# A streaming encoder step on one core: three normalizations, half a choice of experts and two sample steps moved to other places

## The reference

```
h = RMSNorm(x);  z = h @ w_in          # q, k, v of two attentions, forget logits, two gates
o_A = DiffAttn(...); o_B = FoX(...)    # 8 heads each; softmax over earlier frames
x = x + (sig(g_A)*(o_A @ w_pa) + sig(g_B)*(o_B @ w_pb)) @ w_o
# PEER on h2 = RMSNorm(x):
q = h2 @ wq; sc = q . subkeys          # 8 heads x 2 lists of 128 scores
top 16 of each list -> 256 sums -> top 16 of these, softmax g
act = gelu(u[e] . h2);  x = x + sum_e g*act*v[e]     # 128 experts (rows of u and v) per frame
y = RMSNorm_final(x)
```

## Time and profile before

| | us |
|---|---|
| median of 3 runs (2168.32 to 2173.65) | 2169.91 |
| profiled execution | 2172.85 |
| its span | 2171.0 |
| busy: PE / DVE / POOL / ACT | 1649.2 / 1504.9 / 750.6 / 542.9 |
| mean rate of transfers over the span | 347 GB/s |

### The profile page before, as it was taken

The page is one execution under the profiler, slowest core; times in us unless marked ns, Lnnn a source line. Parts: engine busy times, 40 slices in busy tenths (PEclk is TensorE's granted clock), DMA queues, the critical chain, the costliest instruction groups (busy, mean ns, idle before and its releaser), DMA issues.

```text
span 2171.0 us, 22161 instructions
## 1 busy us (share of the span) xinstructions
PE 1649.2 (76%) x7163; PEld 1035.9 (48%) x7163; DVE 1504.9 (69%) x3350; ACT 542.9 (25%) x1451; POOL 750.6 (35%) x697
## 2 busy tenths in 40 slices
PE   7878889898878766988868667977886665666555
PEld 6777886375456522764466323535673222222211
DVE  1121207687877798458976898876789997888786
ACT  2233012111621222145601223733022210001011
POOL 0000000354333334334433334333254455554552
PEclk9988899999979987999989988987999888788878
DMA  7743564799999988999899988897999899999996
GB/s 229 264 140 97 202 229 162 291 421 396 423 369 421 421 347 344 370 387 347 331 417 421 419 300 362 333 410 298 420 379 421 330 413 410 422 421 421 422 403 275
DMA packets 129395, 753.79 MB, mean 347 GB/s; under 512 B 16992, under 2 KB 33296, under 8 KB 42880
## 3 DMA queue, kind: packets, MB, share of 16 engines
q0 software_dynamic: 78336, 570.46, 65.0%
q1 hardware_dynamic: 28432, 155.19, 19.1%
q10 hardware_dynamic: 22512, 26.73, 3.6%
HBM read 732.32 MB, written 19.48 MB: 346 GB/s over the span
## 4 chain that ended last, share of the span: by engine, by line
PE 38%; DMA 25%; DVE 25%; issue 6%; ACT 4%; POOL 1%; ACTq 0%; SPq 0%; DVEq 0%; POOLq 0%; PEldq 0%
DMA ring<-in_uv,stage 17%; PE pz L1249 8%; PE pz L1260 8%; DVE ring L1998 7%; PE acc L1598 7%; DVE vsum L2025 3%; DMA wbuf<-in_w_o 2%; DVE F L1875 2%; PE ps L1556 2%; PE ps L1501 2%; DMA wbuf<-in_w_q 2%; DMA wbuf<-in_w_pa 1%; DMA zt_joint<-F 1%; DVE F L1870 1%; PE ps L1521 1%
## 5 line engine op out<-in xcount | busy, mean ns | idle before, releaser
L804 POOL DMA_INDIRECT ring<-in_uv,stage x544 | 692.9, 1274 | 998.8 <-DVE vsum L2025 350.7
L1598 PE MATMUL acc<-ring,diag 128*128 128x512 f32 (+1 forms) x1112 | 623.0, 707 | 293.0 <-DVE diag L2009 202.9
L1998 DVE CUSTOM_DVE_ANT_0 ring<-ring,xb 128x1024 f32<-128x1024 f32 x544 | 649.3, 1221 | 95.0 <-DMA ring<-in_uv,stage 92.8
L1598 PEld LDWEIGHTS acc<-ring,diag 128*128 128x128 f32 (+1 forms) x1112 | 226.5, 217 | 651.8 <-DVE diag L2009 295.4
L2025 DVE SCALAR_TENSOR_TENSOR vsum<-ring,coefd,vsum 128x1024 f32<-128x1024 f32 x261 | 335.7, 1286 | 10.4 <-DVE coefd L2016 1.2
L1126 ACT ACTIVATE gel<-dots 128x1 f32<-128x1 f32 x544 | 102.0, 200 | 921.1 <-DVE dots L1998 907.0
L822 POOL COPY stage<-idx 128x4 int32<-128x4 int32 x136 | 54.9, 404 | 393.4 <-DVE gw L1944 392.6
L1249 PE MATMUL pz<-F,wbuf 128*128 128x128 f32 (+1 forms) x896 | 171.8, 351 | 9.8 <-PE pz L1249 4.8
L1249 PEld LDWEIGHTS pz<-F,wbuf 128*128 128x128 f32 x896 | 141.9, 200 | 40.0 <-issue 16.0
L2016 DVE TENSOR_SCALAR coefd<-gel,gw 128x1 f32<-128x1 f32 x266 | 55.8, 210 | 111.5 <-ACT gel L1126 111.2
L1260 PE MATMUL pz<-wbuf,F 128*128 128x256 f32 (+1 forms) x384 | 85.0, 381 | 1.9 <-PE pz L1260 1.9
(11 more groups left out here) (381 smaller groups left out, 1943.1 us busy)
## 6 DMA issues: line engine op xcount, KB each, us to landing
wbuf<-in_w_z SPq DMA_DIRECT2D x58, 1024.0 KB, 7.1
wbuf<-in_w_q SPq DMA_DIRECT2D x32, 1024.0 KB, 9.8
wbuf<-in_w_pa SPq DMA_DIRECT2D x16, 1024.0 KB, 10.0
wbuf<-in_w_o SPq DMA_DIRECT2D x16, 1024.0 KB, 10.3
ring<-in_uv,stage POOLq DMA_INDIRECT x544, 12.2
wbuf<-in_w_pb SPq DMA_DIRECT2D x16, 512.0 KB, 8.8
wbuf<-in_w_sk SPq DMA_DIRECT2D x4, 1024.0 KB, 11.0
zt_mid<-F ACTq DMA_DIRECT2D x18, 128.0 KB, 5.3
```

Of the source, the lines that this page charges most:

```text
L804: pool.indirect_dma_start(out=ring[:, slot, :], out_offset=None, in_=d["uv"], in_offset=bass.IndirectOffsetOnAxis(ap=stage[:, a, k:k + 1], ...
L1598: last = nc.tensor.matmul(acc[0:nq, c * 512:(c + 1) * 512], diag[:, parity, 0:nq], ring[:, slot, D + c * 512:D + (c + 1) * 512], start=Fal ...
L1998: nc.vector.tensor_tensor_reduce(out=u, in0=u, in1=xb[:, t % 2, :], scale=1.0, scalar=0.0, op0=ALU.mult, op1=ALU.add, accum_out=dots[:, sl ...
```

## The change

Four parts.

1. Opening. The normalizations and transposes of tiles 2, 3 and 4 leave the opening and stand behind pieces 16 to 19 of tile 0's front (TURN_O and the first three of YPROJ). In the opening only tile 1's stays. TensorE's transposes of tiles 2 to 4 now also wait for the copies of tile 0's attention output, since they use the same two banks.
2. Filling of tile 0's front. The eight gate chunks stand behind pieces 1, 2, 4, 6, 8, 10, 12, 14 (were 0, 2, 4, 6, 8, 10, 11, 13). Of the six query chunks two stand behind pieces 15 and 25, the others behind 35 and later (were 16, 21, 26, 31, 36, 38). EARLY is 3: of group 1's chunks one less (a key chunk) is done before tile 0's slots and one more beside them.
3. Choice of experts of tile 3 in halves. top(3, i) works on four of the eight heads in the front, and the other four are an event late_top between half blocks 2 to 22 of tile 3's own slots; GpSimd and VectorE wait for it before half block 32. The sample's choice moves from half blocks 2 to 42 to 26 to 56. A new area class JointTop lays two halves out.
4. Sample. Piece 4 does step 2, piece 5 step 3, the latter with other banks (ps[0] and pz[0] instead of po); the results are scaled one piece later.

```diff
-EARLY = 4
+EARLY = 3
...
-        return 1.5 if what == "front" and p >= TOP else 1.0
+        return 1.0
...
-    norms = [("bias", 0, 0)]
-    for t in range(1, TILES):
-        norms += [("norm_h", t, 0)] + ([("load_x", t + 1, 0)] if t + 1 < TILES else []) + [("turn_h", t, 0)]
...
+    behind = {0: [("bias", 0, 0)], 1: [("norm_h", 1, 0), ("load_x", 2, 0)], 6: [("turn_h", 1, 0)]}
+    for n, i in enumerate(GROUP_ITEMS[HEADS:]):
+        plan += [("project", 0, i)] + behind.get(n, [])
+
+    gates, queries, keys = ([("project", g, i) for i in items]
+                            for g, items in ((2, GATE_ITEMS), (4, QUERY_ITEMS), (1, KEY_ITEMS[:EARLY])))
+    beside_front = {NORM_O: queries[:1], NORM_X: queries[1:2],
+                    TURN_O: [("norm_h", 2, 0), ("load_x", 3, 0)],
+                    YPROJ: [("turn_h", 2, 0), ("norm_h", 3, 0), ("load_x", 4, 0)],
+                    YPROJ + 1: [("turn_h", 3, 0), ("norm_h", 4, 0)],
+                    YPROJ + 2: [("turn_h", 4, 0), ("keep_h", 1, 0)]}
+    for n, part in enumerate(spread(gates, lambda e: 1.0, NORM_O)):
+        beside_front[n + 1] = part + beside_front.get(n + 1, [])
+    for n, part in enumerate(spread(queries[2:] + keys, lambda e: 11.8 if e[1] == 1 and e[2] else 5.0, PIECES - SCORE)):
+        beside_front[SCORE + n] = part
...
-        if 2 <= b < 2 + 4 * 11 and b % 4 == 2:
-            plan.append(("sample_top", TILES - 1, b // 4))
+        if 2 <= b < 2 + 2 * 11 and b % 2 == 0:
+            plan.append(("late_top", JOINT, b // 2 - 1))
+        if 26 <= b < 26 + 3 * 11 and b % 3 == 2:
+            plan.append(("sample_top", TILES - 1, (b - 26) // 3))
...
+        def sample_tail(u):
+            return ps[0] if u == 3 else po
+        def sample_out(u):
+            return pz[0] if u == 3 else po
...
+                if b == SLOTS // BLOCK // 2 and h == 0 and t == JOINT:
+                    pool.wait_ge(route_ready, t + 2)
...
+                if t > 1:
+                    pe.wait_ge(oT_stored, 3)
...
-                    pe.wait_ge(h_stored, 8 * TILES)
+                    pe.wait_ge(h_stored, 8 * 2)
...
-                elif p == 4:
-                    for u in (2, 3):
-                        turn(u)
-                        pv(u)
+                elif p in (4, 5):
+                    turn(p - 2)
+                    pv(p - 2)
...
-                a, heads = (fa(t), HEADS) if t <= JOINT else (top_s, HEADS // 4)
+                a, heads = (fa(t), HEADS) if t < JOINT else (top_j[half], HEADS // 2) if t == JOINT else (top_s, HEADS // 4)
+                turn = t + half if t <= JOINT else t + 1
```

More of the change, by code:

```diff
@@ L197, in make_plan @@
         plan += [("project", 0, GROUP_ITEMS[i]), ("toeplitz", i, 0)]
-    norms = [("bias", 0, 0)]
-    for t in range(1, TILES):
-        norms += [("norm_h", t, 0)] + ([("load_x", t + 1, 0)] if t + 1 < TILES else []) + [("turn_h", t, 0)]
[L201 to L215, removed]
+    behind = {0: [("bias", 0, 0)], 1: [("norm_h", 1, 0), ("load_x", 2, 0)], 6: [("turn_h", 1, 0)]}
[12 more added lines that the diff above has]
+        beside_front[SCORE + n] = part
+    for p in range(PIECES):
+        plan += [("front", 0, p)] + beside_front.get(p, [])
     for t in range(JOINT):
@@ L536, in build @@
         top_s = SampleTop(F, qT[:, D:D + 4 * P])
+        top_j = [JointTop(F, half) for half in range(2)]
         def fa(t):
@@ L1001, in sample @@
                 u = p - 2
-                for v in (u,) if u in (0, 1) else (2, 3) if u == 2 else ():
+                for v in (u,) if 0 <= u < 4 else ():
                     act.wait_ge(turned, 16 * t + v + 1)
@@ L1444, in pv @@
                                 cols, v_ = slice(0, DVB), vb[0:w, j, h * DVB:(h + 1) * DVB]
-                            last = nc.tensor.matmul(po[DEC * i:DEC * i + DEC, cols],
+                            last = nc.tensor.matmul(sample_out(u)[DEC * i:DEC * i + DEC, cols],
                                                     joint.aTS[0:w, P * j + DEC * i:P * j + DEC * i + DEC], v_,
@@ L1938, in top @@
                                                         a.e12[:, 1, :], ALU.mult, ALU.add))
-                    step(nc.vector.tensor_copy(idx[:, par, 0:slots], a.e12[:, 0, :]))
-                    dve.wait_ge(g_exp, t + 1)
+                    here = slice(half * slots, half * slots + slots)
+                    step(nc.vector.tensor_copy(idx[:, par, here], a.e12[:, 0, :]))
+                    dve.wait_ge(g_exp, turn + 1)
                     gexp = a.cand[:, :, 1, :]
@@ L1943, in top @@
                     step(nc.vector.reciprocal(sstat[:, 0:heads], sst[:, 0:heads]))
-                    nc.vector.tensor_tensor(gw[:, par, 0:slots].rearrange("p (h s) -> p h s", h=heads), gexp,
+                    nc.vector.tensor_tensor(gw[:, par, here].rearrange("p (h s) -> p h s", h=heads), gexp,
                                             sstat[:, 0:heads].rearrange("p (h o) -> p h o", o=1)
@@ L2045, in experts @@
             def experts(t, b, h):
+                if b == SLOTS // BLOCK // 2 and h == 0 and t == JOINT:
+                    dve.wait_ge(route_ready, t + 2)
                 if b == 0 and h == 0:
-                    dve.wait_ge(route_ready, t + 1)
+                    dve.wait_ge(route_ready, t + 1 if t <= JOINT else t + 2)
                     if t == TILES - 1:
@@ L2080, in _ @@
                     sample(p)
+                elif what == "late_top":
+                    top(t, p, 1)
                 elif what == "sample_top":
```

61 lines of the change are left out of this document (37 added, 24 removed).

## The result

The changed kernel takes 2136.85 us in the median of 4 runs (2130.67 to 2143.72) against 2169.17 of before (now also 4 runs): ratio 0.985, 95% interval [0.9825, 0.9875], so 32.5 us (27 to 38) are gone where 15 were forecast. The profiled execution took 2134.4 us, its span is 2132.6, the mean clock 0.903.

The account below looks back on a forecast made before the run. TensorE and chains of small waits bound the time before the first slot, then DMA transfers at about 421 GB/s. Terms 7 + 5 + 3 = 15 us off 2172.85 gave 2157.9, median forecast 2155, range 2135 to 2171.

Parts of the forecast that it names:

- Choice in halves: Tile 3's choice: 8 of 12 us idle transfers regained in tile 2's slots, 5 lost in tile 3's, net 3.
- Opening: Before tile 0's front: moving the transposes of tiles 2 to 4 and unblocking tile 1's saves 10.0 us.
- First attention step: Tile 0's front: qT's load, now bare, costs 5.9 us; of the opening's 10.0 us, 4.9 are left.
- Normalizations beside the output projection: Tile 0's front: query chunk fills a wait, 4 us saved; moved transposes and waits cost more, net about 1 lost.
- Fillings: Query chunks moved from between OPROJ and SCORE to behind SCORE: net 11.3 us saved, about 2 of new waiting.
- Key chunk: One more key chunk beside tile 0's slots: 2.5 us lost if transfers decide, 11.7 if TensorE; taken as 6.
- rival A: Transfers decide everything later: key chunk costs 2.5, sample gives 9, halves 12, tile 3 loses nothing; 2138 us, chance 0.2.
- Sample: Sample's steps in tile 2's slots: both VectorE scaling waits go, 5 us gained of at most 16.4.
- Tile 3's slots: The late half of the choice in tile 3's slots, where VectorE has 23 us idle: 5 us lost (0 to 27).
- rival C: Late half makes VectorE the bound of tile 3's first 44 slots: 12 us slower than before, 2182 us, chance 0.08.

Follow-up runs that it names:

- experiment 4: Changed kernel with tile 3's choice whole again and a choice piece's weight back at 1.5: ratio 0.9952 to the kernel before, 22 us slower than the changed kernel.
- experiment 1: Changed kernel with only a choice piece's weight back at 1.5 in tile 2's list: ratio 0.9888 to the kernel before, 8 us slower than the changed kernel.
- experiment 3: Kernel before with tile 3's choice in halves and the sample's choice later, weight 1.5 kept: ratio 0.9971, 6.3 us faster than before.
- experiment 2: Changed kernel with tile 3's choice whole again, weight 1 kept: ratio 0.9913 to the kernel before, 13.7 us slower than the changed kernel.
- experiment 8: Changed kernel with the sample's piece 4 doing steps 2 and 3 again: ratio 0.9868 to the kernel before, 3.9 us slower than the changed kernel.
- experiment 10: Changed kernel with the first gate chunk behind piece 0 instead of piece 1 of tile 0's front: ratio 0.9821 to the kernel before, median 2131.85 us.
- the repetition: The changed kernel run once more, unchanged: ratio 0.9843 to the kernel before, tile 2's slots 408.3 us.

## Why the prediction was wrong in size

The step that failed is "Choice in halves": 8 of 12 us gained in tile 2's slots, 5 lost in tile 3's, net 3. Undoing the whole part costs 22 us of device time (experiment 4); in the traces tile 2's slots change by 22 us and tile 3's by 3, net 19. That is 16 to 19 us more than the net 3, where 17 were missing.

Two things were wrong in the step. First, I priced only the choice's own 60 us, with 12 us of idle transfers, and the sample's 40 us, with 16; tile 2's slots had 54 us of idle transfers in all, 19 of them in their first quarter, to which the sum gave nothing. Second, the edit also sets a choice piece's weight from 1.5 to 1, and I gave that no term: it takes the choice from fifteen half blocks to eleven and spreads attention, sample and projections over four more. That saves 8 us of device time, and 9 to 17 in the stage ahead of the choice (experiments 1 and 4). How the rest divides is open: halves give net 5 to 6 on the list of before (experiment 3), but 14 by device time on the even list (experiment 2).

The other terms, one by one:

- **Opening**, 10.0 forecast, 7.5 in these two executions, 9.2 if counted from the load of the bias. I wrote that nothing but ScalarE's copies holds the next chunk. The copy itself stands on ScalarE behind the root of tile 1's normalization, which waits for VectorE, which waits for the load of the bias. In the profile after, and the load in the one before:

```profile
77.10 0.48 DVE L1738 MEMSET bias<- 64x512 f32 x1 [52.73 <-DMA bias<-skew]
77.51 0.09 DVE L1701 TENSOR_SCALAR sst<-sst 128x1 f32<-128x1 f32 x1
77.64 0.20 ACT L878 ACTIVATE sstat<-sst 128x1 f32<-128x1 f32 x1 [4.92 <-DVE sst L1701]
```

```profile
75.40 0.48 DVE L1708 MEMSET bias<- 64x512 f32 x1 [51.36 <-DMA bias<-skew]
```

The transposes left TensorE's way; the normalization did not leave ScalarE's. The same wait already stood ahead of the 76.05 that I started from, so it is not what the sum missed: the load ended 1.7 us later in this execution. Over all traces it ends between 72.6 and 77.5 us with the new opening and between 75.4 and 78.6 with the old one; from it to the end of the opening pass 31.5 to 33.0 us with the new and 40.6 to 41.3 with the old, 8 to 10 us less. The size was right.
- **First attention step**: bare load 5.9 us forecast, 7.18 measured; behind it, with 7 us at the halved clock, 14.5 us to the second gate chunk instead of 13.7. Of 4.9 us that were to be left there 0.4 were: 2.5 are missing from the opening, 1.3 from the load, 0.8 from the rest. Experiment 10 confirms from the other side what the bare load costs.
- **Normalizations beside the output projection**: 4 saved by the query chunk, 4.7 spent; TensorE enters the projection 6.3 us earlier than before (232.53 against 238.87) and its second half 1.3 us earlier (263.47 against 264.75), so 4.1 gained on top of the 2.2 of the attention's end, and 5.0 spent. Right.
- **Fillings**: 11.3 forecast; from 1.3 us ahead at 263.47 to 13.7 at the choice is 12.4. Right. Of the 4.5 us that were missing at the second gate chunk, 1.8 came back in the rest of the attention, to which I gave no term, 1.1 here and 0.5 at the forget logits, so that the first dot product comes 12.2 us earlier for 13 forecast. That total is near in part by luck.
- **Key chunk**: 6 forecast, 2 to 3 measured. Transfers decide there, as in rival A; the even tie that I read from TensorE's 19.30 of 20 us was none, since that stretch stays at 421 GB/s with a chunk more.
- **Sample**: 5 forecast, 4 by device time and 5 by the stage on the changed list. Right there; it depends on the list (experiment 8).
- **Tile 3's slots**: 5 lost forecast, 3.3 measured here, 4.3 in experiment 3. Right; rival C's late half does not bind, VectorE keeps 7 of 140 us free.

Rival A forecast the time, with 9 for the sample, 12 for the choice and nothing lost in tile 3. Measured are 5, 22 and 3.3: its number is right by chance. Its principle, that transfers decide, holds for the key chunk and for tile 2's slots, whose whole gain is idle transfer time, but it too looked for that time in the two stretches alone. Tile 1's 4.0 us are within what one kernel's executions differ in there.

## What to carry to other kernels

Where a table of weights spreads work over slots, read an edit of it from the new list first: count the events of each stretch before and after, and price every stretch in which the count changes, not only the one whose events were made cheaper. Sum the idle time of what bounds the stage over the whole of it (here 54 us of transfers), not only over its worst stretches. An instruction that was "moved away" still holds whoever stands behind it on its other engines: follow the chain on each of them. A wait uncovered on TensorE cost its 7.18 us here and about 3 more at the slower clock behind it, so cover it with the chunk that is to come anyway.

## What the runs showed of the hardware

After 7.18 us without a matmul the granted clock was 0.50 for the next 7 us and 1.00 from 123 us on, and so it was, 4.4 us earlier, in the repetition (7.25 us without a matmul); the attention matmuls took 0.80 us instead of 0.49 for four. With a gate chunk in that gap it stayed at 1.00. A 1 MB chunk more in tile 0's slots, where transfers ran at 421 GB/s, cost 2 to 3 us. And in tile 1's first 20 half blocks the same program took 171.5 or 180.4 us, at a clock of 0.94 or 0.91 and 382 or 363 GB/s: what decides between them is open.
